# A hybrid mixer and MoE block: expert weights moved in 3 transfers of 4 MB instead of 12 of 1 MB, from arrays laid out on the host

## What is computed

```
hn = rms_norm(h)                       # h: 272 rows x 1024
proj = hn @ w_in                       # 1024 x 10856, used in column blocks of 512
u = gate0 * (attn @ w_o_attn) + gate1 * (ssm @ w_o_ssm)
h = h + u @ w_out
tok = rms_norm(h)
for e in range(32):                    # w_gate_up[e]: 1024 x 2048, 8 MB; w_down[e]: 1024 x 1024, 4 MB
    gate, up = split(tok @ w_gate_up[e] + b_gate_up[e])
    act = (clip(up) + 1) * (min(gate, 7) * sigmoid(1.702 * min(gate, 7)))
    out += dense_w[:, e] * (act @ w_down[e] + b_down[e])
```

## Time and profile before

| | |
|---|---|
| Time, 3 runs | 1553.04 us median (1550.83 to 1553.22) |
| Span of the profiled execution | 1562.4 us; the profile gives no other time of its own for it |
| Mixer and routing, until the first gate-up matmul | 616.1 us |
| 32 units and the end | 946.3 us |
| TensorE busy | 1455.7 us (93%) |
| Moved by the DMA engines | 468.6 MB, nearly all of it weights |

### The profile page before, as it was taken

One profiled execution on the slowest core, in us unless ns is written; L12 is line 12 of the kernel. 1 busy time (PEld: TensorE's weight loads), 2 busy tenths in 40 slices (PEclk: granted clock), 3 DMA queues, 4 the chain that ended last, 5 costly groups with the idle time before them and its releaser, 6 DMA issues.

```text
span 1562.4 us, 16879 instructions
## 1 busy us (share of the span) xinstructions
PE 1455.7 (93%) x6492; PEld 691.9 (44%) x6492; DVE 357.9 (23%) x878; ACT 230.9 (15%) x488; POOL 51.5 (3%) x37
## 2 busy tenths in 40 slices
PE   6999999998999999999999998999899899899997
PEld 5885664446778864333333322332232233233332
DVE  3555661016220012211211111111211111121111
ACT  3113330122331001100101000100100100010111
POOL 0503210000000000000000000000000000000000
PEclk9999999999998998999999999999999999999998
DMA  9432121371133555999999999999999999999994
GB/s 331 170 118 99 54 67 41 122 256 55 54 109 128 204 200 213 418 417 416 418 417 415 417 418 416 417 418 417 415 418 418 415 417 418 416 416 417 414 418 191
DMA packets 106793, 468.60 MB, mean 300 GB/s; under 512 B 10524, under 2 KB 10676, under 8 KB 73956
## 3 DMA queue, kind: packets, MB, share of 16 engines
q1 hardware_dynamic: 106500, 467.23, 74.9%
q10 hardware_dynamic: 256, 0.85, 0.1%
HBM read 467.01 MB, written 1.05 MB: 300 GB/s over the span
## 4 chain that ended last, share of the span: by engine, by line
PE 55%; DMA 17%; SPq 15%; DVE 6%; issue 2%; ACT 2%; POOL 2%; POOLq 0%; DVEq 0%; ACTq 0%
DMA weights<-in_w_gate_up_dram 16%; PE ps L894 12%; PE ps L918 8%; SPq L383 7%; SPq L379 7%; PE ps L644 6%; PE ps L533 6%; PE ps L769 5%; PE ps L711 3%; PE ps L498 2%; PE ps L563 2%; PE ps L794 2%; PE ps L928 1%; ACT hnT L983 1%; PE ps L747 1%
## 5 line engine op out<-in xcount | busy, mean ns | idle before, releaser
L894 PE MATMUL ps<-weights,hnT 128*64 128x512 f32 x2000 | 448.3, 596 | 29.9 <-DMA weights<-in_w_gate_up_dram 29.9
L894 PEld LDWEIGHTS ps<-weights,hnT 128*64 128x64 f32 x2000 | 136.0, 136 | 337.6 <-issue 247.0
L983 ACT ACTIVATE hnT<-ps 128x512 f32<-128x512 f32 (+1 forms) x96 | 50.5, 526 | 823.2 <-PE ps L498 590.3
L1498 DVE TENSOR_SCALAR ssmT<-ps 128x512 f32<-128x512 f32 x32 | 22.2, 692 | 541.9 <-PE ps L894 541.9
L918 PE MATMUL ps<-weights,hnT 128*64 128x512 f32 x512 | 118.6, 606 | 7.7 <-ACT hnT L983 7.7
L918 PE MATMUL ps<-last_slot,hnT 128*64 128x512 f32 x504 | 113.6, 592 | 0.0
L644 PE MATMUL ps<-weights,hnT 128*128 128x512 f32 x224 | 96.8, 593 | 1.6 <-issue 1.6
L533 PE MATMUL ps<-hnT,weights 128*128 128x272 f32 x384 | 90.7, 399 | 0.3 <-DMA weights<-in_w_in_dram 0.3
L498 PE MATMUL ps<-const,ssmT 128*128 128x128 f32 (+1 forms) x346 | 55.1, 292 | 33.5 <-DVE ssmT L1505 21.0
L533 PEld LDWEIGHTS ps<-hnT,weights 128*128 128x128 f32 x384 | 74.0, 193 | 16.4 <-DMA weights<-in_w_in_dram 0.7
L498 PEld LDWEIGHTS ps<-const,ssmT 128*128 128x128 f32 (+1 forms) x346 | 38.6, 147 | 89.3 <-DVE ssmT L1505 49.2
(11 more groups left out here) (201 smaller groups left out, 1105.0 us busy)
## 6 DMA issues: line engine op xcount, KB each, us to landing
weights<-in_w_gate_up_dram SPq DMA_DIRECT2D x250, 1024.0 KB, 20.3
weights<-in_w_down_dram SPq DMA_DIRECT2D x64, 1024.0 KB, 24.4
last_slot<-in_w_down_dram SPq DMA_DIRECT2D x63, 1024.0 KB, 22.4
weights<-in_w_in_dram SPq DMA_DIRECT2D x21, 2048.0 KB, 8.0
weights<-in_w_o_ssm_dram SPq DMA_DIRECT2D x4, 2048.0 KB, 7.8
arena<-in_w_gate_up_dram SPq DMA_DIRECT2D x5, 1024.0 KB, 10.1
weights<-in_w_o_attn_dram SPq DMA_DIRECT2D x2, 2048.0 KB, 7.9
weights<-in_w_out_dram SPq DMA_DIRECT2D x2, 2048.0 KB, 11.0
```

The source lines that it names most:

```text
L894: mm = pe.matmul(bank(4 + b)[64 * a:64 * a + 64, :], xe[:, 2 * (k % 4) + k // 4, :], w[:, FF * b + 512 * a:FF * b + 512 * a + 512], start= ...
L983: return nc.scalar.activation(o, i, ACT.Copy)
```

## The change

All weights are arranged on the host so that a transfer reads one long run of memory for each partition. A block of the mixer is 128 runs of 16 KB (before: 1024 of 2 KB); the small block S is one transfer of 128 runs of 3.3 KB (before: two, of 1024 runs of 288 bytes and 1024 of 128 bytes). An expert is three transfers of 4 MB, 128 runs of 32 KB each: the first half of gate-up, the second half, and down. `last_slot` becomes the sixth slot of one array, so that down is one region.

With the size of a transfer its waits change. Half of gate-up is reloaded when TensorE has used all 4 of its pieces (before: each piece by itself), down when all 4 of its pairs are used; TensorE starts on a half, or on down, when the whole of it has landed. The held pieces are the same. Where some pieces of a part are held, the part's transfer moves the rest of it (`cols`). For unit 0 the first half waits for OS3 and OA0 to be used up, the second for WO0, down for WO1. The matmuls and all other engines' work are as before.

```diff
+GU_PARTS = 2
+DN_PARTS = 1
-    weights = mem("weights", RING * SLOT)
-    last_slot = mem("last_slot", SLOT)
+    weights = mem("weights", (RING + 1) * SLOT)
+    last_slot = weights[:, RING * SLOT:]
...
-            def load_down(e, i):
-                src = w_down[0, bass.ds(e, 1), 2 * i * P:(2 * i + 2) * P, :].rearrange("e (k p) n -> p (e k) n", p=P)
...
-                sp.dma_start(split(region, 2), src).then_inc(dn_in[i], 16)
-            def load_gate_up(e, k):
-                sp.dma_start(gu_chunk[k], w_gate_up[0, bass.ds(e, 1), k * P:(k + 1) * P, :].rearrange("e p n -> (e p) n")).then_inc(gu_in[k], 16)
+            def load_down(e, i, cols=slice(0, 2 * SLOT)):
+                dst = weights[:, 4 * SLOT + cols.start:4 * SLOT + cols.stop]
+                sp.dma_start(dst, w_down[bass.ds(e, 1), i, :, cols].rearrange("e p n -> (e p) n")).then_inc(dn_in[i], 16)
+            def load_gate_up(e, i, cols=slice(0, 2 * SLOT)):
+                dst = weights[:, 2 * SLOT * i + cols.start:2 * SLOT * i + cols.stop]
+                sp.dma_start(dst, w_gate_up[bass.ds(e, 1), i, :, cols].rearrange("e p n -> (e p) n")).then_inc(gu_in[i], 16)
...
-                for src, a, b in block_source(name):
-                    sp.dma_start(wslot(name)[:, :, a:b], src).then_inc(slot_in[n % RING], 16)
+                if name == "S":
+                    sp.dma_start(weights[:, 0:S_COLS], w_small).then_inc(slot_in[0], 16)
+                else:
+                    at = n % RING * SLOT
+                    sp.dma_start(weights[:, at:at + SLOT], w_blocks[n - 1]).then_inc(slot_in[n % RING], 16)
...
+                for kind, parts, load, freed, counts in (("gu", GU_PARTS, load_gate_up, gu_free, KD), ("dn", DN_PARTS, load_down, dn_free, 4)):
+                    per = KD // parts
+                    for i in range(parts):
+                        need = wanted(u, kind, i, per)
+                        if not need:
+                            continue
+                        ago = 1
+                        while not set(need) & set(wanted(u - ago, kind, i, per)):
+                            ago += 1
+                        sp.wait_ge(freed, (u - ago) * counts + counts // parts * (i + 1))
+                        width = 2 * SLOT // per
+                        load(e, i, slice(width * (need[0] - per * i), width * (need[-1] + 1 - per * i)))
...
-            for k in range(KD):
-                if k == 6:
-                    sp.wait_ge(uT_ok, KD)
-                    load_held(held_gu[3:4])
-                sp.wait_ge(*used_up(("OS3", "OA0", "OA1", "WO0")[k // 2]))
-                load_gate_up(0, k)
+            sp.wait_ge(*used_up("OS3"))
+            sp.wait_ge(*used_up("OA0"))
+            load_gate_up(0, 0)
+            sp.wait_ge(*used_up("OA1"))
+            sp.wait_ge(uT_ok, KD)
+            load_held(held_gu[3:4])
+            sp.wait_ge(*used_up("WO0"))
+            load_gate_up(0, 1)
             sp.wait_ge(*used_up("WO1"))
             load_down(0, 0)
-            load_down(0, 1)
...
+    gate_up = np.asarray(inputs["w_gate_up"])[0].reshape(EXPERTS, GU_PARTS, KD // GU_PARTS, P, 2 * FF)
+    down = np.asarray(inputs["w_down"])[0].reshape(EXPERTS, DN_PARTS, KD // DN_PARTS, P, D)
...
+        "w_gate_up": gate_up.transpose(0, 1, 3, 2, 4).reshape(EXPERTS, GU_PARTS, P, 2 * SLOT),
+        "w_down": down.transpose(0, 1, 3, 2, 4).reshape(EXPERTS, DN_PARTS, P, 2 * SLOT),
```

More of the change, by code:

```diff
@@ L63 @@
 SLOT = KD * 512
+S_COLS = KD * 104
+GU_PARTS = 2
+DN_PARTS = 1
 def constants():
@@ L97, in constants, with build @@
     return np.concatenate([a.astype(np.float32) for a in parts.values()], axis=1), where
-def build(nc, x, meta_tokens, norm1_g, w_in, conv_w, conv_b, dt_bias, a_log, d_skip, ssm_norm_g,
-          w_o_attn, w_o_ssm, w_out, norm2_g, w_router, b_router, w_gate_up, b_gate_up,
-          w_down, b_down, final_g, out):
+def build(nc, x, meta_tokens, norm1_g, w_small, w_blocks, conv_w, conv_b, dt_bias, a_log, d_skip, ssm_norm_g,
+          norm2_g, w_router, b_router, w_gate_up, b_gate_up, w_down, b_down, final_g, out):
     table, where = constants()
@@ L266, in wslot @@
         n = NB[name] % RING
-        return split(weights[:, n * SLOT:(n + 1) * SLOT], KD)
+        return split(weights[:, n * SLOT:n * SLOT + (S_COLS if name == "S" else SLOT)], KD)
     gu_chunk = [split(weights[:, 0:4 * SLOT], KD)[:, k, :] for k in range(KD)]
@@ L308, in build @@
     bias_in, bias_part, gu_free, dn_free = sem("bias_in"), sem("bias_free"), sem("gu_free"), sem("dn_free")
-    gu_in = [sem(f"gu_in{k}") for k in range(KD)]
+    gu_in = [sem(f"gu_in{i}") for i in range(GU_PARTS)]
     held_in = {key: sem("held_in_%d_%s%d" % key) for key in held}
-    dn_in = [sem(f"dn_in{k}") for k in range(4)]
+    dn_in = [sem(f"dn_in{i}") for i in range(DN_PARTS)]
     h2T_dve, h2T_act, wr_ok, count_ok = sem("h2T_dve"), sem("h2T_act"), sem("wr_ok"), sem("count_ok")
@@ L317, in build @@
     codes_ok, sq3, root3, rstd3, out_ok, out_in = sem("codes_ok"), sem("sq3"), sem("root3"), sem("rstd3"), sem("out_ok"), sem("out_in")
[L319 to L334, removed]
     def loaded(eng, name):
         n = NB[name]
-        uses = sum(2 if BLOCKS[m] == "S" else 1 for m in range(n % RING, n + 1, RING))
-        eng.wait_ge(slot_in[n % RING], 16 * uses)
+        eng.wait_ge(slot_in[n % RING], 16 * (n // RING + 1))
     def used_up(name):
@@ L369, in load_held @@
                 for e, kind, i in keys:
-                    for part, rows in zip(held[e, kind, i], (2 * i, 2 * i + 1) if kind == "dn" else (i,)):
-                        w = w_down if kind == "dn" else w_gate_up
-                        sp.dma_start(part, w[0, e, P * rows:P * rows + P, :]).then_inc(held_in[e, kind, i], 16)
-            def load_down(e, i):
-                src = w_down[0, bass.ds(e, 1), 2 * i * P:(2 * i + 2) * P, :].rearrange("e (k p) n -> p (e k) n", p=P)
-                region = weights[:, 4 * SLOT + 2 * D * i:4 * SLOT + 2 * D * (i + 1)] if i < 2 \
-                    else last_slot[:, 2 * D * (i - 2):2 * D * (i - 1)]
-                sp.dma_start(split(region, 2), src).then_inc(dn_in[i], 16)
-            def load_gate_up(e, k):
-                sp.dma_start(gu_chunk[k], w_gate_up[0, bass.ds(e, 1), k * P:(k + 1) * P, :].rearrange("e p n -> (e p) n")).then_inc(gu_in[k], 16)
+                    if kind == "gu":
+                        at = FF * 2 * (i % 4)
+                        sp.dma_start(held[e, kind, i][0], w_gate_up[e, i // 4, :, at:at + 2 * FF]).then_inc(held_in[e, kind, i], 16)
+                    else:
+                        for part, kk in zip(held[e, kind, i], (2 * i, 2 * i + 1)):
+                            sp.dma_start(part, w_down[e, 0, :, D * kk:D * kk + D]).then_inc(held_in[e, kind, i], 16)
+            def load_down(e, i, cols=slice(0, 2 * SLOT)):
[4 more added lines that the diff above has]
+                sp.dma_start(dst, w_gate_up[bass.ds(e, 1), i, :, cols].rearrange("e p n -> (e p) n")).then_inc(gu_in[i], 16)
             for n, name in enumerate(BLOCKS):
@@ L401, in _ @@
                     sp.dma_start(bias_raw, b_gate_up[0]).then_inc(bias_in, 16)
-                for src, a, b in block_source(name):
-                    sp.dma_start(wslot(name)[:, :, a:b], src).then_inc(slot_in[n % RING], 16)
-            def load_expert(u, e, peeled=False):
[L407 to L411, removed]
-                for k in range(KD):
[L414 to L421, removed]
+                if name == "S":
+                    sp.dma_start(weights[:, 0:S_COLS], w_small).then_inc(slot_in[0], 16)
+                else:
+                    at = n % RING * SLOT
+                    sp.dma_start(weights[:, at:at + SLOT], w_blocks[n - 1]).then_inc(slot_in[n % RING], 16)
@@ new lines, in load_expert, with kept_out, wanted @@
+            def load_expert(u, e, peeled=False):
+                def kept_out(v, kind, kk):
+                    return peeled and (("gu", kk) if kind == "gu" else ("dn", kk // 2)) in HELD.get(v, [])
+                def wanted(v, kind, i, per):
+                    return [kk for kk in range(per * i, per * i + per) if not kept_out(v, kind, kk)]
+                for kind, parts, load, freed, counts in (("gu", GU_PARTS, load_gate_up, gu_free, KD), ("dn", DN_PARTS, load_down, dn_free, 4)):
[10 more added lines that the diff above has]
+                        load(e, i, slice(width * (need[0] - per * i), width * (need[-1] + 1 - per * i)))
@@ L423, in _ @@
             sp.wait_ge(aoT_ps, KD)
-            load_down(0, 2)
             load_held(held_dn)
-            for k in range(KD):
-                if k == 6:
-                    sp.wait_ge(uT_ok, KD)
-                    load_held(held_gu[3:4])
-                sp.wait_ge(*used_up(("OS3", "OA0", "OA1", "WO0")[k // 2]))
-                load_gate_up(0, k)
+            sp.wait_ge(*used_up("OS3"))
+            sp.wait_ge(*used_up("OA0"))
+            load_gate_up(0, 0)
+            sp.wait_ge(*used_up("OA1"))
```

(38 more changed lines are left out.)

1 line of the change is left out of this document (removed).

## The result

Four runs of the changed kernel gave 1538.30 us median (1536.83 to 1543.47), the kernel before beside them 1553.13 (1550.83 to 1553.33): a ratio of 0.9895, 95% interval 0.9859 to 0.9931, 14.8 us or 1.0% faster. A second series of six runs, on another chip than the first experiments, gave 0.9918 (0.9900 to 0.9936). Forecast were 1547.0 us and 0.4%, with a range from 1539: the direction was right, the size less than half, and the measured time lies just outside the range.

A forecast was written before the change was run, and what follows sets the result against it. Transfers bound the middle units, the end hanging on unit 26's last gate-up weights. 10.3 us lost less 25.7 x 0.78 saved, and 0.3 from the mixer, gave 1543, or 1550.7 with recording costs; middle 1547.0 us, range 1539 to 1559.

The forecast's parts named there:

- Shift = 10.3 - 25.7 x saving: Move of the end: 10.3 us lost to two longer waits, less 25.7 times the saving per period.
- part 2: Larger pieces in the units: stream starts 5.1 us later, TensorE has 5.2 us more left at the end; together 10.3.
- parts 3 and 4: Unit 0's own loads cost nothing; in the mixer faster blocks stay hidden, gain 0.3 us, bounds 0 and 0.3.
- part 5: Tail behind unit 26: the last transfer has 13 us to spare, so its 4 MB in one piece is hidden.
- part 1: Longer runs in the units: 104 fewer packets per engine and expert at 7.5 ns save 0.78 us, period 29.40.
- the sum's last step, the recorder: Span 9.4 us above the median: perhaps recording slows transfers, giving 1550.7 instead of 1543 us; the middle, 1547.0, taken.
- Given back: Rival: packet price mostly the recorder's, saving 0.3 to 0.5 us eaten by later waits, 1550 to 1555 us; chance 0.20.
- No gain past 8 KB: Rival: transfer rate saturates or rows are cut into 8 KB packets; saving 0.24, shift +4.1, 1557 us; chance 0.12.
- Strides collide: Rival: engines reading at power-of-two distances, 32 KB per partition, slow to 412 GB/s; period 30.54, 1572 us; chance 0.05.
- The clock: Rival: one 1.5 us pause per unit lowers TensorE's clock, 1.7 us more each unit, about 1554 us; chance 0.05.

The follow-up runs named there:

- the first experiments: Follow-up runs beginning with the kernel before, profiled again with no edit: 1553.38 us.
- the short-run kernel: Against the kernel before: transfers of 4 MB, but still runs of 8 KB for gate-up and 4 KB for down; 1564.02 us, ratio 1.0058.
- the new profile of before: The kernel before profiled once more, no edit: 1553.38 us, span 1551.3 us.
- all four profiles with 24 packets: Changed kernel, twice (1538.30, 1541.52 us); kernel with only the experts' transfers changed (1537.16 us); changed kernel without the queue's wait ahead of block X0 (1539.45 us).

## Why the prediction was right and wrong

**Right: what bounds the kernel, and on what the end hangs.** The units were bound by the queue up to unit 26, and the end moved with the moment at which unit 26's last gate-up weights landed. Shift = 10.3 - 25.7 x saving holds when it is fed with the measured saving: 10.3 - 25.7 x 1.02 = -15.9 us. Up to unit 26 the working gives 779.9 + 5.1 - 25.7 x 1.02 = 758.8; the profiles show 758.9 and 759.2. The rest gives 163.1 + 5.2 = 168.3; the short-run kernel shows 168.3, and the changed one 169.9 and 171.6, because the last unit ran partly at half clock in those executions (its down took 8.5 and 9.5 us instead of 7.09).

**Right: part 2, the loss by larger pieces**, 10.3 us worked out and 9.6 measured by itself; **parts 3 and 4**, nothing from unit 0's loads and nothing that can be seen from the mixer; part 5, no wait behind unit 26, though it reads 2.1 us "behind its bias" where the new profile of before has 0.5: the rest was half clock. The queue did not run dry in the units.

**Wrong: the packet price in part 1**, "I take 7.5 ns, the value nearest in size". The periods are 30.18, 29.93, 29.41 and 29.17 us for 128, 96, 48 and 24 packets. From 128 to 96 only the rows of down grow, from 4 to 8 KB, and a packet is worth 7.8 ns: the 7.5 was right for the step it was read from, and 29.94 had been worked out for 8 KB rows alone. What failed was to carry it on to longer runs, of which there was no row: from 96 to 48 packets each is worth 10.8 ns, from 48 to 24 it is 10.0, and 9.8 over all. The saving is 1.02 us a period instead of 0.78, 6.2 us of the end. Why the step from 4 to 8 KB is worth less per packet than the longer ones stays open.

**Wrong: the sum's last step, the recorder.** The span lay 9.4 us above the median, and I gave half of that to a cost of recording on the transfers, a term that no run shows, which cut the forecast's gain from 10 to 6 us. It was an execution with a slower mixer; the profile gave the clue, for the granted clock by stretch falls to 0.86 and 0.85 in the mixer and is 1.00 in the units, and the prediction made no use of it. Without this step alone the forecast would have been 1542.9 us; with 9.8 ns as well it is 1553.04 - 15.9 = 1537.2, against 1538.30 measured. The range was cut too short besides: its low end of 1539 stands for a saving of 0.94 us, while the prediction's own bound, 10 ns a packet (1.04 us; it prints 1.07), was left outside it, and that bound is nearly what came.

**The rivals.** "Given back" stood on the recorder and fell with it: the saving is the same 1.02 us in all four profiles with 24 packets. "No gain past 8 KB" is refuted by 29.93 against 29.17. "Strides collide": 431 GB/s at 32 KB between partitions, 420 at 64 KB with short runs; none at these distances. "The clock": one pause of 1.03 us per unit left the halves behind it at 7.09 us in the waiting units of the changed kernel. The rival was not groundless: after pauses of 2.0 us, with short runs, 8 of 15 halves took 1.7 us more, as the rival had it, and a pause of 8 us did the same; but such 1.7 us are lost in the next pause where the queue sets a period of 30.16 us.

The estimate from the 425 GB/s of the Trainium skill (DMA: Bandwidth & Descriptors, Measured) was a period of 29.61 us; the trace shows 431 GB/s and 29.17.

## What to carry to other kernels

Where a queue of large transfers is full and sets the pace, count the packets of each engine: here each cost about 10 ns from 8 KB up to 32 KB runs, 3.4% of the rate between 128 and 24 per expert, while nine transfers and completions fewer per expert gave 0.03 us at most. Run length and transfer size are two changes: a part can only be refilled when all of it is used, and used when all of it has landed, so in this kernel each larger part takes its share back at the first refill and at the last landing, and where it leaves nothing to overlap with, as gate-up in one transfer of 8 MB, it takes more than all of the gain. Before a span is compared with a median, look at the clock of the stretches that the change does not touch.

## What was not expected of the hardware

The price of a packet hardly falls with its size: from 96 to 48 packets (8 to 16 KB) 10.8 ns each, from 48 to 24 (16 to 32 KB) 10.0, so that the queue reaches 431 GB/s with 32 KB runs. Pauses of TensorE of 1.0 to 1.3 us before the second half of gate-up left its granted clock at 1.00; after pauses of 2.0 us it ran part of the next matmuls at half clock in 8 cases of 15. Two executions of the same kernel differed by 7.8 us in a part in which no transfer binds, by how much of it TensorE ran at half clock.
